# Moving the two widest score blocks of a pair of heads between the two turns of the pair before it

## The chip, the cores and the metric

The kernel runs on one core of a Trainium2 chip. The metric is the device time of one execution in microseconds (us), smaller is better. The time of the kernel before is the median of three runs.

## The reference

The program computes two blocks of a transformer on 512 tokens of width 1024, in fp32. The first block projects the normalised input, runs two attentions of eight heads each on parts of the projection, multiplies their outputs by a gate and projects them back. The second block is four layers, each with an attention and a feed-forward part; the change does not touch it. Cut to the first block's attentions:

```python
def chunk_causal_attention(q, k, v, pos):        # heads of "phase 1", width 96
    def block(args):
        logits = jnp.einsum('bqhd,bshd->bhqs', qb, k).astype(jnp.float32) * scale
        mask = pos[None, :] < chunk_limit(pb)[:, None]
        logits = jnp.where(mask[None, None], logits, NEG_INF)
        p = jax.nn.softmax(logits, axis=-1).astype(v.dtype)
        return jnp.einsum('bhqs,bshd->bqhd', p, v)
...
def indexer_sparse_attention(q, k, v, q_idx, k_idx, w_idx, pos):   # heads of "phase 2", width 64
    ...
        _, sel = lax.top_k(score, topk)          # each query keeps 128 keys
    ...
        logits = jnp.where(valid[:, None], logits, NEG_INF)
        p = jax.nn.softmax(logits, axis=-1).astype(v.dtype)
        return jnp.einsum('bhqk,bqkhd->bqhd', p, v_sel)
...
    mixed = jnp.concatenate([o_a.reshape(B, S, A_WIDTH) * jax.nn.silu(g_a),
                             o_b.reshape(B, S, B_WIDTH) * jax.nn.silu(g_b)], axis=-1)
    h = h + mixed @ w_out[l]
```

## The kernel before

Every engine runs a program of its own, in an order written out by hand, and the engines wait for each other through counting semaphores. An engine never skips an instruction that waits: what stands behind it waits too.

The first block's attention (`attn`) works on eight pairs of heads, p = 0 to 7. Pairs 0 to 3 are phase 1, pairs 4 to 7 (`p >= PAIRS_B`) phase 2. In phase 2 the two heads j = 0, 1 of a pair lie in the two halves of the partitions of one tile `qp` and one tile `kp`, and the mask of chosen keys is added to the scores. A pair passes through these steps:

1. `prep` (TensorE, L723): four transposes of queries and four of keys into two banks of PSUM. VectorE (`take_heads`, L1965) scales them out of PSUM into `qp` and `kp`.
2. `scores` (TensorE, L767): eight blocks, for each 128 queries i = 0 to 3 and each head j; block i is 128 (i + 1) keys wide. In phase 2 they come in the order of i, j = 0 and j = 1 next to each other. VectorE (L1996, shown as `e<-ring,mask`) adds the mask, takes the maximum of each row and writes the block to SBUF as `e_1[p % 2][j]`.
3. `exps` (ScalarE, L1426): exp of each of the eight blocks, with the sum of each row. VectorE (`take_reciprocal`, L2003) inverts the sums of head j once its blocks are through. Head 0 is scaled by VectorE itself (`normalise`, L2009, four instructions), head 1 by GpSimd (L1143, four instructions).
4. `turn(p, j)` (TensorE, L931): ten transposes of head j's scaled blocks into the PSUM tile `turn`. ScalarE (`take_turned`, L1433) copies them to SBUF as `at_1[j]`. There is one tile `turn`, so the next turn waits for this copy.
5. `pv` (TensorE, L783): the sum over keys, for both heads, into the PSUM tile `out`. VectorE (`gate`, L2017) multiplies it by the gate into `ot`; ScalarE (`out_high`, L1437) rounds that to `o1h`; VectorE (`low`, L2022) makes the rest, `o1l`.

Steps of different pairs are interleaved. In step s of the loop TensorE does `scores(s)`, `pv(s-2)`, `turn(s-1, 0)`, `prep(s+1)`, `turn(s-1, 1)`. VectorE does the score blocks of s, `take_reciprocal(s, 0)`, `normalise(s)`, `take_prep(s+1)`, `take_reciprocal(s, 1)`, `low(s-3)`, `gate(s-2)`. ScalarE does `exps(s)`, `take_turned(s-1, 0)`, `out_high(s-3)`, `take_turned(s-1, 1)`.

PSUM banks are handed out by a ring of four, `ring[n % 4]`, where n is the number of a unit: a score block or half a prep, numbered in the order of `pair_units()`. TensorE may write unit n once VectorE has taken unit n - 4:

```python
    def wait_unit_free(b, k):
        if b.at("unit_taken", k) >= 4:
            pe.wait_ge(m["unit_taken"], b.at("unit_taken", k) - 3)
```

So the fifth block of a pair waits until VectorE has taken its first.

After the last pair's scores there is nothing left to interleave but the output projection. `work.fill(n)` issues n quanta of it, each of three matmuls 512 columns wide (L472); a quantum k needs `low(k)`. In step 8 TensorE does `pv(6)`, `turn(7, 0)`, five quanta, `turn(7, 1)`, six quanta, and in step 9 `pv(7)` and then all other quanta.

Of the kernel before, what the change touches and what calls it, by code (L numbers as in the profile page):

```python
# [101 lines left out]
PAIRS = 8  # L102
PAIRS_B = B_HEADS // 2
# [8 lines left out]


def pair_preps(p):


    return [(x, j) for j in range(2 if p < PAIRS_B else 1) for x in ("q", "k")]


def pair_units():  # L120
    order = [("gate", 6), ("prep", 0, *pair_preps(0)[-1]), ("gate", 7)]
    for p in range(PAIRS):
        order += [("score", p, *u) for u in pair_scores(p)]
        if p + 1 < PAIRS:
            order += [("prep", p + 1, *u) for u in pair_preps(p + 1)]
    return {u: n for n, u in enumerate(order)}

# [348 lines left out]
def tensor_program(pe, m, st, plan):  # L476
# [269 lines left out]
    def attn(b, ob):  # L746
# [9 lines left out]

        def scores(p):
            taken = UNITS[("prep", p, *pair_preps(p)[-1])] + 1 if p else 0
            pe.wait_ge(m["unit_taken"], b.at("unit_taken", taken))
            for j, i in pair_scores(p):  # L760
                if p < PAIRS_B:
                    q, k = m.qp[j][0:B_QK, :], m.kp[j][0:B_QK, :]
                else:
                    half = slice(64 * j, 64 * j + 64)
                    q, k = m.qp[0][half, :], m.kp[0][half, :]
                n = CAUSAL_W[i]
                pe.matmul(bank(("score", p, j, i))[:, 0:n], q[:, i * P:(i + 1) * P], k[:, 0:n],  # L767
                          start=True, stop=True).then_inc(m["unit_ready"], 1)
# [21 lines left out]
        for s in range(PAIRS + 2):  # L790
            if s < PAIRS:
                scores(s)
            if s >= 2:
# [3 lines left out]
            if s + 1 < PAIRS:  # L797
                if s + 1 == PAIRS_B:
                    pe.wait_ge(m["q_normed"], 4)
                prep(s + 1)  # L800
            elif s == PAIRS:
                work.fill(5)
            if 1 <= s < PAIRS + 1:
# [292 lines left out]
    for name in plan:  # L1096
        b = st[name]
# [111 lines left out]
def scalar_program(act, m, d, st, plan, n_pieces):  # L1209
# [211 lines left out]
    def attn(b):  # L1421
        def exps(p):
            for j, i in pair_scores(p):
                act.wait_ge(m["unit_taken"], b.at("unit_taken", UNITS[("score", p, j, i)] + 1))
# [18 lines left out]
        for s in range(PAIRS + 3):  # L1443
            if s >= PAIRS:
                out_high(s - 3)
            if s < PAIRS:
                exps(s)
            if 1 <= s < PAIRS + 1:
                take_turned(s - 1, 0)
            if 3 <= s < PAIRS:  # L1450
                out_high(s - 3)
            if 1 <= s < PAIRS + 1:
                take_turned(s - 1, 1)
# [199 lines left out]
def vector_program(dve, m, st, plan):  # L1653
# [303 lines left out]
    def take_heads(b, unit, p, x, j):  # L1957
        dst = (m.qp if x == "q" else m.kp)[j]
        wait_unit(b, unit)
# [27 lines left out]
    def attn(b):  # L1987
        def scores(p):

            for j, i in pair_scores(p):  # L1990
                if p >= 2:
# [23 lines left out]
        def gate(p):  # L2015
            dve.wait_ge(m["pv_done"], b.at("pv_done", p + 1))
            dve.tensor_tensor(m.ot[p % 2][:], m.out[:], m.gate[:, (p + 4) % 8, :], ALU.mult).then_inc(m["o_taken"], 1)  # L2017

# [12 lines left out]
        for s in range(PAIRS + 3):  # L2031
            if s < PAIRS:
                scores(s)
            if s >= PAIRS:
                low(s - 3)
            if s == 0:

                take_prep(1)
                make_mask()
            if s < PAIRS:  # L2040
                take_reciprocal(s, 0)
                normalise(s)
            if 1 <= s < PAIRS - 1:
                take_prep(s + 1)
            if s < PAIRS:
                take_reciprocal(s, 1)
            if 3 <= s < PAIRS:
                low(s - 3)
            if 2 <= s < PAIRS + 2:
                gate(s - 2)  # L2050
# [502 lines left out]
```

## Time and profile before

| what | value |
| --- | --- |
| median of 3 runs | 2704.96 us |
| lowest and highest | 2703.01 and 2705.85 us |
| the profiled execution's own time | 2703.59 us |
| its span, first to last instruction | 2701.8 us |
| TensorE busy | 2653.8 us (98%) |
| VectorE, ScalarE, GpSimd busy | 1456.8, 1116.9, 1168.1 us |
| phase 2 of the attention in the span | about 268 to 310 us |

Busy time is the time in which the profiler saw an instruction of the engine at work. A matmul's end is modelled, and successive matmuls overlap, so where two matmuls follow without a wait, the distance of their starts is the time that one takes. In a timeline the number in brackets is how long the engine sat idle before the row, and the name behind the arrow is what ended that. PE is TensorE, DVE VectorE, ACT ScalarE, POOL GpSimd. Names of tiles stand without their numbers.

### The profile page before, as it was taken

Reading aid. Unit: us, or ns where it says so; the run is one execution under the profiler, and the core shown is the slowest. Engines: PE = TensorE matmul, PEld = TensorE weight load, DVE = VectorE, ACT = ScalarE, POOL = GpSimd, SP = SyncE. Lnnn points to the kernel's source line nnn. Section 1 sums busy time; section 2 is a strip of 40 time slices with the busy share of each in tenths; the row PEclk is TensorE's granted clock in tenths of the full one; section 3 lists DMA queues with packets and bytes.
Section 4 is the critical chain, followed back from the end, with each engine's and each line's share of the span. In section 5 each row is a group of like instructions: output and inputs, shape, how many; then the busy total and the mean of one; then the engine's idle time right before and its main releaser. Section 6 shows DMA issues by size and latency. Waiting matters only on the chain.

```text
span 2701.8 us, 32030 instructions
## 1 busy us (share of the span) xinstructions
PE 2653.8 (98%) x12868; PEld 2124.2 (79%) x12868; DVE 1456.8 (54%) x2610; ACT 1116.9 (41%) x1509; POOL 1168.1 (43%) x880
## 2 busy tenths in 40 slices
PE   8999999999999999999999999999999999999997
PEld 7786677778888877778888876888888777888886
DVE  5888556657554145657554145575522565565522
ACT  4545544443333236654333236443332444443331
POOL 3454343335445532335445541354455332454453
PEclk9999999999999999999999999999999999999999
DMA  4224032222223321112323331222233221222232
GB/s 163 78 94 172 10 124 86 78 79 94 94 94 109 110 83 62 63 63 96 107 94 109 109 110 48 79 94 105 98 110 109 95 85 71 94 94 96 106 111 78
DMA packets 45605, 253.44 MB, mean 94 GB/s; under 512 B 4560, under 2 KB 9184, under 8 KB 17936
## 3 DMA queue, kind: packets, MB, share of 16 engines
q1 hardware_dynamic: 34656, 232.18, 24.5%
q10 hardware_dynamic: 10800, 19.20, 2.1%
q8 instruction: 102, 1.67, 0.2%
q14 instruction: 47, 0.39, 0.0%
HBM read 249.21 MB, written 10.55 MB: 96 GB/s over the span
## 4 chain that ended last, share of the span: by engine, by line
PE 92%; DVE 4%; ACT 2%; POOL 1%; issue 1%; DMA 0%; SPq 0%; DVEq 0%; ACTq 0%
PE ring L472 78%; PE ring L926 3%; PE turn L931 2%; PE turn L472 1%; PE out L970 1%; POOL wlo L1166 1%; PE ring L636 1%; PE ring L767 1%; PE out L783 1%; DVE sp L2158 1%; PE out L976 0%; DVE e L2126 0%; PE out L1058 0%; DVE z L2161 0%; ACT whi L1217 0%
## 5 line engine op out<-in xcount | busy, mean ns | idle before, releaser
L1166 POOL TENSOR_TENSOR wlo<-raw,whi 128x512 fp32r<-128x512 f32 x840 | 1122.8, 1369 | 1461.2 <-ACT whi L1217 1461.2
L472 PE MATMUL ring<-xh,whi 128*128 128x512 f32 x1888 | 753.0, 399 | 9.1 <-DVE xl L1673 8.2
L472 PE MATMUL ring<-xh,wlo 128*128 128x512 f32 x1888 | 736.4, 390 | 0.0
L472 PE MATMUL ring<-xl,whi 128*128 128x512 f32 x1888 | 736.2, 390 | 0.0
L1217 ACT ACTIVATE whi<-raw 128x2048 fp32r<-128x2048 f32 x215 | 411.3, 1914 | 435.4 <-DMA raw<-in_pieces 419.9
L472 PEld LDWEIGHTS ring<-xh,whi 128*128 128x128 f32 x1888 | 354.9, 188 | 114.3 <-issue 40.9
L472 PEld LDWEIGHTS ring<-xh,wlo 128*128 128x128 f32 x1888 | 354.9, 188 | 74.9
L472 PEld LDWEIGHTS ring<-xl,whi 128*128 128x128 f32 x1888 | 355.1, 188 | 72.6 <-issue 3.4
L2274 DVE SCALAR_TENSOR_TENSOR taps<-u,conv,taps 128x511 f32<-128x511 f32 (+1 forms) x344 | 294.5, 900 | 18.4 <-ACT taps L1615 16.0
L2288 DVE TENSOR_TENSOR u<-ring,r 128x512 f32<-128x512 f32 x168 | 114.4, 687 | 300.9 <-PE ring L472 300.9
L2262 DVE TENSOR_TENSOR h<-ring,h 128x512 f32<-128x512 f32 x72 | 49.6, 689 | 420.0 <-PE ring L852 376.9
L1615 ACT ACTIVATE taps<-u,conv 128x512 f32<-128x512 f32 x172 | 137.9, 809 | 306.6 <-DVE u L2288 306.4
L472 PE MATMUL ring<-hh,whi 128*128 128x512 f32 x672 | 261.4, 389 | 0.0
L472 PE MATMUL ring<-hl,whi 128*128 128x512 f32 x672 | 261.4, 389 | 0.0
L472 PE MATMUL ring<-hh,wlo 128*128 128x512 f32 x672 | 261.4, 389 | 0.0
L472 PE MATMUL ring<-whi,xh 128*128 128x256 f32 (+1 forms) x576 | 181.6, 315 | 1.3 <-POOL wlo L1166 1.3
L472 PE MATMUL ring<-wlo,xh 128*128 128x256 f32 (+1 forms) x576 | 173.6, 301 | 0.0
L472 PE MATMUL ring<-whi,xl 128*128 128x256 f32 (+1 forms) x576 | 173.6, 301 | 0.0
L472 PEld LDWEIGHTS ring<-hl,whi 128*128 128x128 f32 x672 | 126.2, 188 | 26.2
L472 PEld LDWEIGHTS ring<-hh,wlo 128*128 128x128 f32 x672 | 126.2, 188 | 26.2
L472 PEld LDWEIGHTS ring<-hh,whi 128*128 128x128 f32 x672 | 126.1, 188 | 26.2
L472 PEld LDWEIGHTS ring<-whi,xh 128*128 128x128 f32 x576 | 110.4, 192 | 21.1 <-issue 13.9
(285 smaller groups left out, 3355.0 us busy)
## 6 DMA issues: line engine op xcount, KB each, us to landing
raw<-in_pieces SPq DMA_DIRECT2D x215, 1024.0 KB, 4.7
toep<-diag_store ACTq DMA_DIRECT2D x16, 512.0 KB, 3.6
diag_store<-diag_row ACTq DMA_DIRECT2D x1, 5120.0 KB, 25.2
band_store<-band_row ACTq DMA_DIRECT2D x1, 3072.0 KB, 32.5
h<-in_x SPq DMA_DIRECT2D x4, 512.0 KB, 6.7
wbias<-band_store ACTq DMA_DIRECT2D x4, 512.0 KB, 7.4
result<-h SPq DMA_DIRECT2D x8, 256.0 KB, 2.2
raw<-in_pieces SPq DMA_DIRECT2D x4, 256.0 KB, 6.9
```

The lines of the kernel that those rows point to most:

```text
L472: ins = pe.matmul(out, stationary, moving, start=first and n == 0, stop=last and n == 2)
L636: ins = pe.matmul(out, x[:, tok], weights[slot][:, w], start=begins, stop=ends)
L767: pe.matmul(bank(("score", p, j, i))[:, 0:n], q[:, i * P:(i + 1) * P], k[:, 0:n], start=True, stop=True).then_inc(m["unit_ready"], 1)
L783: ins = pe.matmul(m.out[64 * j:64 * j + 64, kk * P:S], v[:, kk, c:c + 64], m.at_1[j][:, at:at + S - kk * P], start=kk == 0, stop=kk == TT - 1)
L926: pe.matmul(m.ring[2 + j][:, 0:n], qs[part, i * P:(i + 1) * P], ks[part, lo:lo + n], start=True, stop=True).then_inc(m["su_ready"], 1)
L931: ins = pe.transpose(m.turn[:, to:to + P], src[:, at:at + P], m.ident[:])
L1166: ins = pool.tensor_tensor(m.wlo[slot][:, part], m.raw[slot][:, part], m.whi[slot][:, part].bitcast(F32), ALU.subtract)
L1217: act.activation(m.whi[p % SLOTS][:], m.raw[p % SLOTS][:], ACT.Copy).then_inc(m["hi_done"], 1)
L1615: act.activation(taps[g][:], m.u[g][:], ACT.Identity, scale=cols[:, 4 * g + 2:4 * g + 3], bias=cols[:, 4 * g + 3:4 * g + 4]).then_inc(m["t ...
L2262: dve.tensor_tensor(m.h[:, k, :], ring(b, k)[:], m.h[:, k, :], ALU.add).then_inc(m["unit_taken"], 1)
L2274: dve.scalar_tensor_tensor(y[:, shift:S], m.u[g][:, 0:S - shift], cols[:, tap:tap + 1], y[:, shift:S], ALU.mult, ALU.add).then_inc(m[signa ...
L2288: dve.tensor_tensor(m.u[g][:], ring(b, 2 * t + g)[:], m.r[:], ALU.mult).then_inc(m["unit_taken"], 1)
```

## The change

In phase 2 a pair's eight score blocks are split. The first six (128, 256 and 384 keys wide) stay where they were, the last two (512 keys wide, "the late blocks") move behind `prep(s+1)` on TensorE, ahead of `turn(s-1, 1)`. The units are numbered anew to match. Queries and keys of odd pairs of phase 2 go to a second place, `qp[1]` and `kp[1]`, since `prep(s+1)` is now taken while scores of s are still to be made. ScalarE's two late exps move between its two copies. On VectorE `gate(s-2)` and `take_prep(s+1)` move ahead of the late blocks, and so ahead of `take_reciprocal(s, 0)` and `normalise(s)`. In step 8 two of the five quanta move ahead of `pv(6)`. `gate` names a semaphore that VectorE's own order has met already.

```diff
--- before.py
+++ after.py
@@ -111,6 +111,16 @@
     return [(j, i) for i in range(TT) for j in range(2)]
 
 
+def first_scores(p):
+
+
+    return pair_scores(p)[:8 if p < PAIRS_B else 6]
+
+
+def late_scores(p):
+    return pair_scores(p)[len(first_scores(p)):]
+
+
 def pair_preps(p):
 
 
@@ -120,9 +130,10 @@
 def pair_units():
     order = [("gate", 6), ("prep", 0, *pair_preps(0)[-1]), ("gate", 7)]
     for p in range(PAIRS):
-        order += [("score", p, *u) for u in pair_scores(p)]
+        order += [("score", p, *u) for u in first_scores(p)]
         if p + 1 < PAIRS:
             order += [("prep", p + 1, *u) for u in pair_preps(p + 1)]
+        order += [("score", p, *u) for u in late_scores(p)]
     return {u: n for n, u in enumerate(order)}
 
 
@@ -754,15 +765,15 @@
             for x, j in pair_preps(p):
                 turn_heads(bank(("prep", p, x, j)), p, x, j)
 
-        def scores(p):
+        def scores(p, blocks):
             taken = UNITS[("prep", p, *pair_preps(p)[-1])] + 1 if p else 0
             pe.wait_ge(m["unit_taken"], b.at("unit_taken", taken))
-            for j, i in pair_scores(p):
+            for j, i in blocks:
                 if p < PAIRS_B:
                     q, k = m.qp[j][0:B_QK, :], m.kp[j][0:B_QK, :]
                 else:
                     half = slice(64 * j, 64 * j + 64)
-                    q, k = m.qp[0][half, :], m.kp[0][half, :]
+                    q, k = m.qp[p % 2][half, :], m.kp[p % 2][half, :]
                 n = CAUSAL_W[i]
                 pe.matmul(bank(("score", p, j, i))[:, 0:n], q[:, i * P:(i + 1) * P], k[:, 0:n],
                           start=True, stop=True).then_inc(m["unit_ready"], 1)
@@ -789,7 +800,9 @@
         gate(b, UNITS[("gate", 7)], 0, 1)
         for s in range(PAIRS + 2):
             if s < PAIRS:
-                scores(s)
+                scores(s, first_scores(s))
+            if s == PAIRS:
+                work.fill(2)
             if s >= 2:
                 pv(s - 2)
             if 1 <= s < PAIRS + 1:
@@ -799,7 +812,9 @@
                     pe.wait_ge(m["q_normed"], 4)
                 prep(s + 1)
             elif s == PAIRS:
-                work.fill(5)
+                work.fill(3)
+            if s < PAIRS and late_scores(s):
+                scores(s, late_scores(s))
             if 1 <= s < PAIRS + 1:
                 turn(s - 1, 1)
             if s == PAIRS:
@@ -1419,8 +1434,8 @@
         take(11)
 
     def attn(b):
-        def exps(p):
-            for j, i in pair_scores(p):
+        def exps(p, blocks):
+            for j, i in blocks:
                 act.wait_ge(m["unit_taken"], b.at("unit_taken", UNITS[("score", p, j, i)] + 1))
                 row = m.e_1[p % 2][j][:, BLOCK_OFF[i]:BLOCK_OFF[i] + CAUSAL_W[i]]
                 act.activation(row, row, ACT.Exp, bias=m.nmax[:, p % 2, j, i:i + 1], scale=-1.0,
@@ -1444,11 +1459,13 @@
             if s >= PAIRS:
                 out_high(s - 3)
             if s < PAIRS:
-                exps(s)
+                exps(s, first_scores(s))
             if 1 <= s < PAIRS + 1:
                 take_turned(s - 1, 0)
             if 3 <= s < PAIRS:
                 out_high(s - 3)
+            if s < PAIRS:
+                exps(s, late_scores(s))
             if 1 <= s < PAIRS + 1:
                 take_turned(s - 1, 1)
 
@@ -1955,7 +1972,7 @@
                 pick_round(8 + (unit if unit[0] == "gate" else GATES[n - 1])[1])
 
     def take_heads(b, unit, p, x, j):
-        dst = (m.qp if x == "q" else m.kp)[j]
+        dst = (m.qp if x == "q" else m.kp)[j if p < PAIRS_B else p % 2]
         wait_unit(b, unit)
         if p < PAIRS_B:
             gain = m.cols[0:B_QK, C_HEAD + (x == "k"):C_HEAD + (x == "k") + 1]
@@ -1985,9 +2002,9 @@
         own.settle()
 
     def attn(b):
-        def scores(p):
-
-            for j, i in pair_scores(p):
+        def scores(p, blocks):
+
+            for j, i in blocks:
                 if p >= 2:
                     dve.wait_ge(m["turned"], b.at("turned", 2 * p - 2 if p >= PAIRS_B else 2 * (p - 2) + j + 1))
                 k, n = UNITS[("score", p, j, i)], CAUSAL_W[i]
@@ -2014,6 +2031,8 @@
 
         def gate(p):
             dve.wait_ge(m["pv_done"], b.at("pv_done", p + 1))
+            if p >= 2:
+                dve.wait_ge(m["ol_ready"], b.at("ol_ready", p - 1))
             dve.tensor_tensor(m.ot[p % 2][:], m.out[:], m.gate[:, (p + 4) % 8, :], ALU.mult).then_inc(m["o_taken"], 1)
 
         def low(p):
@@ -2030,23 +2049,28 @@
         dve.wait_ge(m["gate_ready"], 8)
         for s in range(PAIRS + 3):
             if s < PAIRS:
-                scores(s)
+                scores(s, first_scores(s))
             if s >= PAIRS:
                 low(s - 3)
             if s == 0:
 
                 take_prep(1)
                 make_mask()
+            if PAIRS_B <= s < PAIRS:
+                gate(s - 2)
+                if s < PAIRS - 1:
+                    take_prep(s + 1)
+                scores(s, late_scores(s))
             if s < PAIRS:
                 take_reciprocal(s, 0)
                 normalise(s)
-            if 1 <= s < PAIRS - 1:
+            if 1 <= s < PAIRS_B:
                 take_prep(s + 1)
             if s < PAIRS:
                 take_reciprocal(s, 1)
             if 3 <= s < PAIRS:
                 low(s - 3)
-            if 2 <= s < PAIRS + 2:
+            if 2 <= s < PAIRS_B or PAIRS <= s < PAIRS + 2:
                 gate(s - 2)
 
     def take_v(b, unit, v, half):
```

**VectorE, from pair 4's blocks of 384 keys to pair 5's first block, before.** `e_100` and `e_101` are heads 0 and 1 of an even pair, `e_110` and `e_111` of an odd one; `o1l5` is `low` of pair 1 and `ot0` is `gate` of pair 2.

```order
L1996 ISA e_101_156,nmax_123<-ring3,mask_154 128x384
...
L1996 ISA e_100_155,nmax_123<-ring0,mask_154 128x512
...
L1996 ISA e_101_156,nmax_123<-ring1,mask_154 128x512
...
L2003 RECIPROCAL rl_125<-lsum_124 128x4
...
L2009 TENSOR_SCALAR e_100_155<-e_100_155,rl_125 128x512
L1965 TENSOR_SCALAR qp0_133<-ring2 128x512
L1965 TENSOR_SCALAR kp0_135<-ring3 128x512
L2003 RECIPROCAL rl_125<-lsum_124 128x4
L2022 TENSOR_TENSOR o1l5_174<-ot1_144,o1h5_166 128x512
L2017 TENSOR_TENSOR ot0_143<-out,gate_86 128x512
L1996 ISA e_110_157,nmax_123<-ring0,mask_154 128x128
```

After the change:

```order
L2013 ISA e_101_156,nmax_123<-ring3,mask_154 128x384
...
L2036 TENSOR_TENSOR ot0_143<-out,gate_86 128x512
L1982 TENSOR_SCALAR qp1_134<-ring0 128x512
L1982 TENSOR_SCALAR kp1_136<-ring1 128x512
L2013 ISA e_100_155,nmax_123<-ring2,mask_154 128x512
...
L2013 ISA e_101_156,nmax_123<-ring3,mask_154 128x512
...
L2020 RECIPROCAL rl_125<-lsum_124 128x4
...
L2026 TENSOR_SCALAR e_100_155<-e_100_155,rl_125 128x512
L2020 RECIPROCAL rl_125<-lsum_124 128x4
L2041 TENSOR_TENSOR o1l5_174<-ot1_144,o1h5_166 128x512
L2013 ISA e_110_157,nmax_123<-ring0,mask_154 128x128
```

The two instructions that take queries and keys (`qp`, `kp`) and the gate (`ot0`) now stand ahead of the late blocks. Between the late blocks and the next pair's first block stand the two reciprocals, the scaling and `low`, and nothing else.

**TensorE, from pair 4's turn of head 0 to pair 6's first block, before.** `e_100` and `e_101` are pair 4's heads, `at_10` and `at_11` their turned copies.

```order
L931 MATMUL turn<-ident_62,e_100_155 128x128 x10
L723 MATMUL ring0<-ident_62,q_a_82 128x128 x4
L723 MATMUL ring1<-ident_62,k_a_83 128x128 x4
L931 MATMUL turn<-ident_62,e_101_156 128x128 x10
L767 MATMUL ring2<-kp0_135,qp0_133 128x128
L767 MATMUL ring3<-kp0_135,qp0_133 128x128
```

After, at the same place; here the two rows of L778 with 512 columns are pair 5's late blocks:

```order
L946 MATMUL turn<-ident_62,e_100_155 128x128 x10
L734 MATMUL ring2<-ident_62,q_a_82 128x128 x4
L734 MATMUL ring3<-ident_62,k_a_83 128x128 x4
L778 MATMUL ring0<-kp1_136,qp1_134 128x512
L778 MATMUL ring1<-kp1_136,qp1_134 128x512
L946 MATMUL turn<-ident_62,e_101_156 128x128 x10
L778 MATMUL ring2<-kp0_135,qp0_133 128x128
L778 MATMUL ring3<-kp0_135,qp0_133 128x128
```

The late blocks stand between the two turns, and pair 6's queries and keys go to a place that pair 5's late blocks don't read.

**TensorE, from pair 6's turn of head 0 to pair 7's turn of head 1, before.** Rows of L472 are quanta of the output projection, three rows each; between the first and last `out` rows lie `pv(6)`'s others.

```order
L931 MATMUL turn<-ident_62,e_100_155 128x128 x10
L931 MATMUL turn<-ident_62,e_101_156 128x128 x10
L783 MATMUL out<-at_10_159,v_a_84 64x512
...
L783 MATMUL out<-at_11_160,v_a_84 64x128
L931 MATMUL turn<-ident_62,e_110_157 128x128 x10
L472 MATMUL ring0<-o1h4_165,whi0_55 128x512
L472 MATMUL ring0<-o1l4_173,whi0_55 128x512
...
L472 MATMUL ring0<-o1h0_161,wlo0_58 128x512
L931 MATMUL turn<-ident_62,e_111_158 128x128 x10
```

After:

```order
L946 MATMUL turn<-ident_62,e_100_155 128x128 x10
L778 MATMUL ring2<-kp1_136,qp1_134 128x512
L778 MATMUL ring3<-kp1_136,qp1_134 128x512
L946 MATMUL turn<-ident_62,e_101_156 128x128 x10
L483 MATMUL ring0<-o1h4_165,whi0_55 128x512
...
L483 MATMUL ring0<-o1h5_166,wlo0_58 128x512
L794 MATMUL out<-at_10_159,v_a_84 64x512
...
L794 MATMUL out<-at_11_160,v_a_84 64x128
L946 MATMUL turn<-ident_62,e_110_157 128x128 x10
L483 MATMUL ring0<-o1h6_167,whi0_55 128x512
...
L483 MATMUL ring0<-o1h0_161,wlo0_58 128x512
L946 MATMUL turn<-ident_62,e_111_158 128x128 x10
```

Two late blocks now stand between the turns of pair 6, and two quanta ahead of `pv(6)`; three quanta are left between the turns of pair 7.

## Rows read from the trace of the kernel before

**Rows 1.** The page: its head, and the chain that ended last, by engine.

```profile
span 2701.8 us, 32030 instructions
...
PE 92%; DVE 4%; ACT 2%; POOL 1%; issue 1%; DMA 0%; SPq 0%; DVEq 0%; ACTq 0%
```

**Rows 2.** TensorE's timeline, 284 to 322 us: start, length, engine, line, operation, idle.

```profile
290.20 2.38 PE L783 MATMUL out<-at,v_a 128*64 128x512 f32 x16
292.50 1.31 PE L931 MATMUL turn<-ident,e 128*128 128x128 f32 x10
293.65 0.60 PE L723 MATMUL ring<-ident,q_a 128*128 128x128 f32 x4
294.08 0.60 PE L723 MATMUL ring<-ident,k_a 128*128 128x128 f32 x4
295.14 1.31 PE L931 MATMUL turn<-ident,e 128*128 128x128 f32 x10 [0.45 <-ACT at L1433]
...
301.63 1.31 PE L931 MATMUL turn<-ident,e 128*128 128x128 f32 x10
304.27 1.31 PE L931 MATMUL turn<-ident,e 128*128 128x128 f32 x10 [1.33 <-ACT at L1433]
306.91 2.38 PE L783 MATMUL out<-at,v_a 128*64 128x512 f32 x16 [1.33 <-ACT at L1433]
...
310.28 0.47 PE L472 MATMUL ring<-o1h,whi 128*128 128x512 f32 x1
...
313.81 1.25 PE L931 MATMUL turn<-ident,e 128*128 128x128 f32 x10
```

**Rows 3.** The timeline of all engines, 287 to 290.3 us, same columns.

```profile
287.88 0.29 DVE L1996 CUSTOM_DVE_ANT_0 e<-ring,mask 128x128 f32<-128x128 f32 x1
...
288.23 1.21 PEld L767 LDWEIGHTS ring<-kp,qp 64*128 64x128 f32 x8 [0.46 <-DVE nmax L1996]
...
289.29 0.56 DVE L1996 CUSTOM_DVE_ANT_0 e<-ring,mask 128x384 f32<-128x384 f32 x1 [0.20 <-PE ring L767]
```

**Rows 4.** The timeline of VectorE, 285 to 304 us, same columns.

```profile
286.50 0.69 DVE L2022 TENSOR_TENSOR o1l<-ot,o1h 128x512 fp32r<-128x512 f32 x1
287.11 0.68 DVE L2017 TENSOR_TENSOR ot<-out,gate 128x512 f32<-128x512 f32 x1
...
292.27 0.18 DVE L2003 RECIPROCAL rl<-lsum 128x4 f32<-128x4 f32 x1 [0.72 <-ACT e L1426]
...
297.01 0.29 DVE L1996 CUSTOM_DVE_ANT_0 e<-ring,mask 128x128 f32<-128x128 f32 x1
...
301.40 0.18 DVE L2003 RECIPROCAL rl<-lsum 128x4 f32<-128x4 f32 x1 [0.72 <-ACT e L1426]
...
302.81 0.17 DVE L2003 RECIPROCAL rl<-lsum 128x4 f32<-128x4 f32 x1
```

**Rows 5.** The timeline of ScalarE, 285 to 317 us, same columns.

```profile
291.44 0.71 ACT L1426 ACTIVATE e<-e,nmax 128x512 f32<-128x512 f32 x1
...
302.98 1.24 ACT L1433 ACTIVATE at<-turn 128x1280 f32<-128x1280 f32 x1 [0.91 <-PE turn L931]
304.12 0.62 ACT L1437 ACTIVATE o1h<-ot 128x512 fp32r<-128x512 f32 x1
```

**Rows 6.** The timeline of all engines, 260 to 262.4 us, same columns.

```profile
260.85 0.69 DVE L1996 CUSTOM_DVE_ANT_0 e<-ring,chunk 128x512 f32<-128x512 f32 x1 [0.29 <-PE ring L767]
...
261.58 0.72 ACT L1426 ACTIVATE e<-e,nmax 128x512 f32<-128x512 f32 x1 [0.28 <-DVE nmax L1996]
```

**Rows 7.** The timeline of GpSimd, 301 to 310 us, same columns.

```profile
303.07 4.27 POOL L1143 TENSOR_SCALAR e<-e,rl 128x128 f32<-128x128 f32 x4 [2.60 <-DVE rl L2003]
```

**Rows 8.** The timeline of TensorE, 104 to 109 us, same columns.

```profile
104.70 0.47 PE L636 MATMUL ring<-whi,ct_h 128*128 128x512 f32 x1 [1.27 <-issue]
```

**Rows 9.** Busy time by stretch: bounds, length, each engine's busy us, granted clock, DMA.

```profile
107.40:110.90 3.50, 3.50 (x12) 2.85 (x11) 2.82 (x7) 0.85 (x4) 0.00 (x0) 0.51 0.00 0
...
302.00:309.00 7.00, 4.34 (x33) 2.80 (x33) 3.18 (x7) 3.59 (x5) 4.27 (x4) 1.00 0.00 0
```

## The prediction

> **What bounds the kernel now.** I read the page first: TensorE holds 92% of the chain that ended last [rows 1], so what this stretch gains or loses reaches the end in full, if TensorE is what gains or loses. Then the timeline of TensorE over phase 2, to find where it stands still. A step there is 9.13 us long (from one pair's first block on VectorE to the next pair's, 287.88 and 297.01) [rows 3, 4]. TensorE stands still twice in it: 0.45 us ahead of the turn of head 1, for ScalarE's copy of head 0 [rows 2], and 0.46 us ahead of the pair's fifth score block, for VectorE to take the first one and free its bank [rows 3]. Past the last pair's scores nothing lies between the turns and two waits for the copy stand open, 1.33 us each [rows 2]. Last I read VectorE's timeline for what it does around its waits. The first stall and the last two are what late blocks and quanta can cover; the second one hangs on where VectorE stands when a pair begins, and that is what the change moves.
>
> **The change part by part.** Nothing is added but the second place for queries and keys, which costs no instruction. The count on every engine stays; only order and waits move. So the cost is that of the new loop of waits.
>
> *From a pair's late blocks to the next pair's fifth block.* I follow one step from L, the start of the late blocks on TensorE.
> - To VectorE's work on the first late block. The fifth block, 384 wide, takes 1.06 from TensorE's start (288.23) to VectorE's (289.29) [rows 3]. `pv` makes 1280 columns for two heads side by side in 2.30 (290.20 to 292.50), 0.23 per 128 columns [rows 2]. A block's matmul is made in two passes over its columns. With 128 columns more it lands between 1.06 (none of them counts) and 1.29 (all 0.23 do); I take the middle, 1.17.
> - VectorE to ScalarE's exp of that block: 0.73, from a place where ScalarE stood waiting for exactly this (260.85 to 261.58) [rows 6].
> - exp to the reciprocal of head 0: 0.83 (291.44 to 292.27) [rows 4, 5].
> - Reciprocal, four scalings, reciprocal of head 1: 1.41 (301.40 to 302.81), the second reciprocal 0.17 [rows 4]. The exp of head 1 starts 0.71 after the first [rows 5] and is ready in time.
> - `low`: 0.61 to the next instruction (286.50 to 287.11); from an instruction of this form to a score block it is 0.77 (287.11 to 287.88) [rows 3, 4]. I take 0.70.
> - The next pair's first block on VectorE to TensorE's fifth: 0.35 (287.88 to 288.23) [rows 3].
>
> Together 1.17 + 0.73 + 0.83 + 1.41 + 0.17 + 0.70 + 0.35 = 5.36 us. TensorE needs from L only the late blocks (4 x 0.23 = 0.92), the turn of head 1 (1.15, as 292.50 to 293.65) and the next pair's four small blocks (128, 128, 256, 256 wide, heads side by side: 3 x 0.23 = 0.69) [rows 2]: it arrives at 2.8 and stands still for some 2.5 us. Behind it in TensorE's queue is `pv`, so nothing fills that.
>
> *From the fifth block to the next late blocks.* Before, the eight-block sequence takes 1.97 from the fifth block to `pv` (288.23 to 290.20) [rows 2, 3]: 0.69 for the 384-wide pair, 0.92 for the 512-wide one, and 0.36 for banks that come free one by one. The 512-wide pair leaves this place; I leave the 0.36 here: 1.05 (bounds 0.69 and 1.1). Then `pv` 2.30, the turn of head 0 1.15, two halves of prep at 0.43 (293.65 to 294.08) [rows 2]: 1.05 + 2.30 + 1.15 + 0.86 = 5.36.
>
> So the new period is 5.36 + 5.36 = 10.72 us against 9.13: 1.59 more. The loop closes three times, from pair 4 to 5, 5 to 6 and 6 to 7; pair 4 begins as before, since the step ahead of it is not changed. 3 x 1.59 = +4.77 us at the start of pair 7. The 0.45 wait for the copy is gone, covered by the late blocks, and it gains nothing: it lay inside a step that is now as long as the chain through VectorE.
>
> Other waits inside the step, counted from F, the pair's first block on VectorE. ScalarE begins the copy of head 0 1.35 after its turn starts (301.63 to 302.98), then `out_high` 1.14 later and 0.62 long [rows 2, 5], so it is free at 0.35 + 1.05 + 2.30 + 1.35 + 1.14 + 0.62 = 6.81; the late exp is wanted at 0.35 + 5.36 + 1.17 + 0.73 = 7.61. Hidden in steps 4 to 6. GpSimd's scaling of head 1 starts 0.26 after its reciprocal and takes 4.27 here [rows 4, 7]; it would be through well ahead of its turn, a step later. Both have room only because the step is longer.
>
> *The tail, from F of pair 7.* The turn of pair 6's head 0 starts at 0.35 + 1.05 + 2.30 = 3.70, the late blocks (no prep now) at 4.85, VectorE has them at 6.02, the exp could start at 6.75, ScalarE is free at 6.81. The second exp starts 0.71 later and is done, with its row sums, 0.83 after that: 8.35. Only then can ScalarE copy the turn of head 1, and `pv(6)` follows 1.29 after the copy's start (302.98 to 304.27, the same distance from copy to TensorE) [rows 2, 5]: 9.64. Before it is 306.91 - 297.01 = 9.90 [rows 2, 4]. So two waits of 1.33 are filled with 0.92 and two quanta, and of that just 0.26 shows ahead of `pv(6)`, since the copy itself is now late. The two quanta count behind it: five take 3.53 (310.28 to 313.81) [rows 2], so 2 x 0.71 = 1.41 less work remains. The tail gives 0.26 + 1.41 = 1.67. The three quanta left between pair 7's turns, 2.12, still cover a copy of 1.35. GpSimd's scaling for pair 7 ends near 6.81 + 0.83 + 1.41 + 0.26 + 4.27 = 13.6, its turn comes near 15: no wait.
>
> *The sum.* +4.77 - 1.67 = +3.1 us. The profiled execution, 2703.59 us, would become 2706.7; it lies 1.4 below the median of its three runs, 2704.96, so for the median I say 2708.1.
>
> **What hides what, and the clock.** A stall of 2.5 us is longer than any that TensorE has in phase 2 now. The trace shows the granted clock at 0.51, that is 1.2 GHz, from 107.4 to 110.9 after a 1.27 us gap at 103.4 with thin work behind it [rows 8, 9]; yet over 302 to 309, with two gaps of 1.33 and 4.34 of 7 us busy, it stayed at 1.00, 2.4 GHz [rows 2, 9]. So gaps alone don't decide here and the new stall lies on the unsafe side of both. The Trainium skill, page "TensorE: Matmul & The Clock Gate", section "Why this matters for your kernels", puts the danger at idle gaps longer than this one would be; by it the clock holds and the sum stays +3.1. The drop at 107.4 does not fit that rule. A drop of 3.5 us at half speed costs up to 1.7 us where TensorE's own work is on the chain, and half of the new period is TensorE's.
>
> **Rivals.**
> 1. *The clock falls behind one or more of the three stalls.* Each costs between 0.9 and 1.7 us: one gives 2709.4, three up to 2713.2. For it: the gap at 104.70. Against it: 302 to 309 [rows 2, 8, 9].
> 2. *The other side: the stall does not form, and the covered waits show.* It takes VectorE reaching the next pair's first block early enough, that is the path of 5.36 us down to TensorE's 2.8. Then a step loses its 0.45 and 0.46: 3 x 0.91 = 2.7, one more 0.45 in step 4, and the tail of 1.67: -4.9, so 2700.1 us. The point from which it decides: the total is nil when the path is 1.0 us shorter, 4.3 us (3 x 1.0 = 3.1), and faster below. For it: VectorE idles 0.72 per step for exps now [rows 4], a sign of some room. Against it: each piece is a measured distance with its wait in place, and none looks 1 us too long.
> 3. *ScalarE or GpSimd becomes the wait as well.* If ScalarE got to the late exps as late in each step as in pair 7, nothing changes, it has 0.8 us of room (7.61 - 6.81); were the copies 1 us later the period would grow by 0.2, in all +0.6: 2708.7. Little speaks for it.
>
> **How the numbers follow.** A change of under 0.2% (5.4 us) is about what this kernel's measurement can't tell from none; the three runs spread over 2.8 us. Chances: the stall with the clock held 63%, with a clock drop 22%, rival 2 in full or part 10%, rival 3 5%. With the bounds of the steps (1.06 or 1.29; 0.61 or 0.77; 0.69 or 1.1) the period lies between 10.2 and 11.0, the total between +1.4 and +4, and with the spread of medians the likeliest case by itself spans 2706.0 to 2709.6. The range of 8 in 10 adds one or two drops above and a partly smaller stall below: 2704.6 to 2711.6. Slower by over 0.2% (2710.4) needs two drops, 0.15; faster by over 0.2% (2699.5) needs more than rival 2, 0.03.
>
> **What would show each step.** In the changed profile: a period of 10.7 in phase 2 between first blocks of pairs on VectorE; TensorE idle some 2.5 us ahead of the fifth block of pairs 5, 6 and 7, ended by VectorE's row maximum; no wait ahead of the turn of head 1 in steps 4 to 6; VectorE idle twice around the late blocks, ended by TensorE and by ScalarE's exp; `pv(6)` still waiting about 0.7 for ScalarE's copy. It is wrong if the period is below 9.5, or if the stall stands at another block.

## The result, and the profile after

The changed kernel takes 2709.88 us in the median of 22 runs (2707.28 to 2715.25), the one before 2705.30 us in the median of 22 runs on the same chips (2700.96 to 2708.90). The ratio is 1.0018, with a 95% interval of 1.0012 to 1.0024: slower by about 4.9 us (3.2 to 6.5). That is clear of zero, and small: 0.18% of the time. The profiled execution took 2711.00 us. From the page, its head and the chain by engine:

```profile
span 2709.2 us, 32040 instructions
...
PE 92%; DVE 4%; ACT 2%; POOL 1%; issue 1%; DMA 0%; DVEq 0%; SPq 0%; ACTq 0%
```

The chain's shares are those of before [rows 1], so they don't show the difference; the timelines do. Here is TensorE over one step of the changed kernel, from pair 4's first block to pair 5's `pv`. L778 are score blocks, L946 turns, L734 preps, L794 `pv`.

```profile
269.99 2.11 PE L778 MATMUL ring<-kp,qp 64*128 64x128 f32 x12
272.02 2.38 PE L794 MATMUL out<-at,v_b 128*64 128x512 f32 x16
274.33 1.31 PE L946 MATMUL turn<-ident,e 128*128 128x128 f32 x10
275.48 0.60 PE L734 MATMUL ring<-ident,q_a 128*128 128x128 f32 x4
...
276.44 1.13 PE L778 MATMUL ring<-kp,qp 64*128 64x512 f32 x4
277.50 1.31 PE L946 MATMUL turn<-ident,e 128*128 128x128 f32 x10
278.74 1.03 PE L778 MATMUL ring<-kp,qp 64*128 64x128 f32 x8
281.71 1.75 PE L778 MATMUL ring<-kp,qp 64*128 64x384 f32 x4 [1.93 <-DVE nmax L2013]
283.39 3.38 PE L794 MATMUL out<-at,v_b 128*64 128x512 f32 x16
```

The late blocks stand at 276.44, between prep and the turn of head 1, and the wait of 0.45 us ahead of that turn [rows 2] is gone. Pair 5's four small blocks start at 278.74. Then TensorE idles 1.93 us by its matmuls, until VectorE has taken the first block. The 0.46 at this place before [rows 3] was read from the record of the weight loads, where the same wait is now 2.33:

```profile
281.71 0.61 PEld L778 LDWEIGHTS ring<-kp,qp 64*128 64x128 f32 x4 [2.33 <-DVE nmax L2013]
```

VectorE in the same step:

```profile
270.62 0.29 DVE L2013 CUSTOM_DVE_ANT_0 e<-ring,mask 128x128 f32<-128x128 f32 x1
...
277.71 0.69 DVE L2013 CUSTOM_DVE_ANT_0 e<-ring,mask 128x512 f32<-128x512 f32 x1 [0.31 <-PE ring L778]
...
279.30 0.18 DVE L2020 RECIPROCAL rl<-lsum 128x4 f32<-128x4 f32 x1 [0.27 <-ACT e L1441]
...
280.70 0.17 DVE L2020 RECIPROCAL rl<-lsum 128x4 f32<-128x4 f32 x1
280.78 0.66 DVE L2041 TENSOR_TENSOR o1l<-ot,o1h 128x512 fp32r<-128x512 f32 x1
281.36 0.28 DVE L2013 CUSTOM_DVE_ANT_0 e<-ring,mask 128x128 f32<-128x128 f32 x1
```

and ScalarE's first late exp:

```profile
278.45 0.72 ACT L1441 ACTIVATE e<-e,nmax 128x512 f32<-128x512 f32 x1 [1.01 <-DVE nmax L2013]
```

This is the loop of the prediction, row by row: late block on TensorE 276.44, on VectorE 277.71, its exp 278.45, the reciprocal 279.30, the second reciprocal 280.70, `low` 280.78, the next pair's first block 281.36, TensorE's fifth block 281.71. Pair 4's first block stood at 270.62, so the period is 10.74 us.

The next two periods are 12.38 each (first blocks at 281.36, 293.74, 306.12), 1.64 more. In the step of pair 5 the time from the fifth block to `pv` is 1.68 us (281.71 to 283.39) instead of 1.05, and `pv` takes 3.3 us instead of 2.3; in the step of pair 6 `pv` alone takes 3.9 (295.14 to 299.08). Busy time by stretch, the granted clock in the column before the last two:

```profile
278.70:282.10 3.40, 1.47 (x12) 1.02 (x12) 3.10 (x14) 2.80 (x8) 1.14 (x2) 0.99 0.00 0
282.10:285.50 3.40, 3.40 (x10) 0.98 (x10) 1.50 (x8) 2.76 (x11) 3.40 (x3) 0.50 0.00 0
...
295.70:299.10 3.40, 3.40 (x17) 1.31 (x13) 0.49 (x4) 1.43 (x6) 2.26 (x2) 0.50 0.00 0
```

For 3.4 us from 282.1 and again from 295.7 the clock is granted at 0.50, the level of 1.2 GHz. TensorE had been busy 1.47 of the 3.4 us ahead of the first fall.

The two traces differ ahead of this stretch too: from 238 to 241 us the clock of the changed kernel stood at 0.50 and that of before at 1.00, and pair 4's first block comes at 270.62 instead of 269.61. So the stretch from that block on is compared, and not the whole span.

The tail, TensorE from the turn of pair 6's head 0:

```profile
309.82 1.31 PE L946 MATMUL turn<-ident,e 128*128 128x128 f32 x10
311.06 1.13 PE L778 MATMUL ring<-kp,qp 64*128 64x512 f32 x4
312.46 1.31 PE L946 MATMUL turn<-ident,e 128*128 128x128 f32 x10 [0.27 <-ACT at L1448]
...
315.76 2.38 PE L794 MATMUL out<-at,v_a 128*64 128x512 f32 x16 [0.60 <-ACT at L1448]
...
326.63 2.37 PE L794 MATMUL out<-at,v_a 128*64 128x512 f32 x16
```

The two waits of 1.33 us [rows 2] are down to 0.27 and 0.60. `pv(6)` comes 9.64 us behind pair 7's first block (306.12) and `pv(7)` 10.87 behind `pv(6)`; before it was 9.90, and 12.22 (306.91 to 319.13).

The places that all runs are compared by, in us, each from its own timelines of VectorE and TensorE. F is the first block of a pair on VectorE; the last column counts the falls of the clock between F of pair 4 and `pv(7)`.

| kernel | F of pair 4 to 5, 5 to 6, 6 to 7 | F of 7 to pv(6) | pv(6) to pv(7) | F of 4 to pv(7) | clock falls |
| --- | --- | --- | --- | --- | --- |
| before | 9.13, 9.14, 9.13 | 9.90 | 12.22 | 49.52 | 0 |
| changed | 10.74, 12.38, 12.38 | 9.64 | 10.87 | 56.01 | 2 |
| changed, again | 10.74, 12.38, 10.74 | 11.33 | 10.86 | 56.05 | 2 |
| spare matmuls | 10.75, 10.74, 10.74 | 9.64 | 10.86 | 52.73 | 0 |
| low later | 10.17, 10.13, 10.13 | 9.62 | 10.86 | 50.91 | 0 |
| next pair first | 8.79, 9.12, 9.12 | 9.97 | 10.85 | 47.85 | 0 |
| copy between | 8.80, 9.41, 9.16 | 9.91 | 11.63 | 48.91 | 0 |
| last pair only | 9.13, 9.14, 9.13 | 9.66 | 10.85 | 47.91 | 0 |
| quanta only (both runs) | 9.13, 9.13, 9.14 | 9.90 | 10.85 | 48.15 | 0 |
| scores only | 10.75, 10.74, 12.37 | 9.64 | 13.96 | 57.46 | 2 |

### The profile page after: what moved, and what is told of

Its sections match the earlier page's. It is cut to its first block, busy times and chain, and to the rows that moved or that the text cites. A ratio compares the mean times of both kernels' runs of the same rounds, so it can differ in the third digit from the quotient of the medians.

```text
span 2709.2 us, 32040 instructions
## 1 busy us (share of the span) xinstructions
PE 2658.9 (98%) x12868; PEld 2124.5 (78%) x12868; DVE 1459.5 (54%) x2610; ACT 1117.8 (41%) x1509; POOL 1168.3 (43%) x880
## 3 DMA queue, kind: packets, MB, share of 16 engines
q8 instruction: 102, 1.67, 0.2%
## 4 chain that ended last, share of the span: by engine, by line
PE 92%; DVE 4%; ACT 2%; POOL 1%; issue 1%; DMA 0%; DVEq 0%; SPq 0%; ACTq 0%
PE ring L483 78%; PE ring L941 3%; PE turn L946 2%; PE turn L483 1%; PE out L985 1%; POOL wlo L1181 1%; PE ring L778 1%; PE ring L647 1%; PE out L794 1%; DVE sp L2182 1%; PE out L991 0%; DVE e L2150 0%; PE out L1073 0%; DVE z L2185 0%; ACT whi L1232 0%
## 5 line engine op out<-in xcount | busy, mean ns | idle before, releaser
L1635 ACT ACTIVATE taps<-taps 128x512 f32<-128x512 f32 x88 | 55.7, 633 | 175.5 <-DVE taps L2298 175.5
```

The lines of the kernel that those rows point to most:

```text
L1635: act.activation(taps[0][0:rows, :], taps[0][0:rows, :], ACT.Silu).then_inc(m["silu"], 1)
```

## Experiments

Theory A is the prediction's: a loop of waits from a pair's late blocks through VectorE, ScalarE's exp and VectorE again to the next pair's fifth block. Its rivals are named in each expectation. Distances in the traces repeat to 0.02 us where the order is the same and the clock holds, while whole runs of one kernel spread over some 8 us. So a cause is read from the traces, and the ratio says what it is worth.

**The next pair's blocks first.** VectorE's order alone is altered (cut to the main place):

```diff
             if s < PAIRS:
-                scores(s, first_scores(s))
+                scores(s, first_scores(s)[2 if s > PAIRS_B else 0:])
...
             if s < PAIRS:
                 take_reciprocal(s, 0)
+            if PAIRS_B <= s < PAIRS:
+                if s + 1 < PAIRS:
+                    scores(s + 1, first_scores(s + 1)[:2])
+                take_reciprocal(s, 1)
+            if s < PAIRS:
                 normalise(s)
...
```

> The changed kernel, with VectorE's order altered alone: behind a pair's late blocks it inverts the sums of head 0, takes the next pair's first two blocks, inverts the sums of head 1, and only then scales head 0 and makes low. Theory A (the stall is VectorE's order: reciprocal, scaling and low ahead of the next pair's first block): the fifth block can start 1.17 + 0.73 + 0.83 + 0.22 + 0.35 = 3.3 us after the late blocks instead of 5.36, TensorE gets there at 2.8 to 2.9, so the stall falls from 2.3 to some 0.4 us and the period from 10.7 to 8.7 us, under the 9.13 of before; in all 3 x -0.43 and the tail's -1.7, about -3.0 us against before, and no fall of the clock in phase 2. Theory B (the late blocks themselves are what costs, by TensorE's work or by the banks, whatever VectorE does): the period stays above 10 us and the time some 3 us above before.

Ratio to before 0.9997 (0.9988 to 1.0005), median 2703.61 us. TensorE with its weight loads, then VectorE, then ScalarE, in the step of pair 7:

```profile
293.22 1.13 PE L778 MATMUL ring<-kp,qp 64*128 64x512 f32 x4
...
295.52 2.15 PE L778 MATMUL ring<-kp,qp 64*128 64x128 f32 x12
297.92 2.38 PE L794 MATMUL out<-at,v_a 128*64 128x512 f32 x16 [0.25 <-ACT at L1448]
```

```profile
296.54 0.51 PEld L778 LDWEIGHTS ring<-kp,qp 64*128 64x128 f32 x4 [0.39 <-DVE nmax L2013]
```

```profile
295.10 0.69 DVE L2013 CUSTOM_DVE_ANT_0 e<-ring,mask 128x512 f32<-128x512 f32 x1
...
296.07 0.18 DVE L2020 RECIPROCAL rl<-lsum 128x4 f32<-128x4 f32 x1 [0.27 <-ACT e L1441]
296.19 0.29 DVE L2013 CUSTOM_DVE_ANT_0 e<-ring,mask 128x128 f32<-128x128 f32 x1
```

```profile
295.94 0.71 ACT L1441 ACTIVATE e<-e,nmax 128x512 f32<-128x512 f32 x1
...
296.65 1.21 ACT L1448 ACTIVATE at<-turn 128x1280 f32<-128x1280 f32 x1
```

The wait ahead of the fifth block fell from 2.33 to 0.39 us by the weight loads, as expected, and the period from 10.74 to 9.12 (8.79 in the first step). So theory A holds and B is out: with the late blocks left where they are, VectorE's order alone takes the loss away. The size was missed, 9.12 for 8.7. TensorE now waits 0.25 us ahead of `pv` for ScalarE's copy, which stands behind both late exps: exp at 295.94, copy at 296.65, `pv` at 297.92. This is a second loop, through ScalarE: from the late blocks to `pv` 4.70 us (293.22 to 297.92), from `pv` to the next late blocks 4.42 (288.80 to 293.22), together the 9.12. It was close behind the first, and the expectation had not summed it.

**`low` later.** `low(s - 4)` goes ahead of `gate(s - 2)`, and the old place is left out but for the last pair:

```diff
             if PAIRS_B <= s < PAIRS:
+                if s > PAIRS_B:
+                    low(s - 4)
                 gate(s - 2)
...
-            if 3 <= s < PAIRS:
+            if 3 <= s < PAIRS_B or s == PAIRS - 1:
                 low(s - 3)
```

> The changed kernel with low of a pair moved behind the next pair's first six blocks on VectorE, ahead of the gate. Theory A (every VectorE instruction between the late blocks and the next pair's first block is on the loop, at its full length): the period falls by 0.58 us, from 10.74 to 10.16, the stall from 2.3 to 1.7; in all 1.7 us less than the changed kernel, +1.3 to +1.5 against before if the clock holds, up to +3 if it falls once. Theory B: VectorE's order is not the limit, no change against the changed kernel (+4.6).

Ratio 1.0009 (1.0000 to 1.0018), median 2706.74 us. TensorE around the stall:

```profile
288.07 1.03 PE L778 MATMUL ring<-kp,qp 64*128 64x128 f32 x8
290.43 1.12 PE L778 MATMUL ring<-kp,qp 64*128 64x384 f32 x4 [1.33 <-DVE nmax L2013]
```

The period is 10.13 to 10.17 and the wait 1.33: an instruction of 0.58 us taken off the loop gave 0.57 to 0.61 of period and 0.60 of stall. From F of pair 4 to `pv(7)` it is 1.39 us over before, as expected, with no fall of the clock in this trace.

**Spare matmuls in the stall.** They compute nothing that is used; `pv` overwrites them.

```diff
             for j, i in blocks:
+                if p > PAIRS_B and (j, i) == (0, 2):
+                    pe.wait_ge(m["o_taken"], b.at("o_taken", p - 2))
+                    for _ in range(2):
+                        pe.matmul(m.out[:], m.ident[:], m.chunk[:], start=True, stop=True)
```

> The changed kernel with two spare matmuls of 512 columns (0.92 us each by pv's rate) on TensorE ahead of the fifth block of pairs 5, 6 and 7, into the tile out, which pv overwrites. They lie inside the stall of 2.3 us. Theory A (the clock falls because of the stall, and this is the part of the loss beyond 3.1 us): no stretch at 0.50 in phase 2, all three periods at 10.7 us, time about 3.0 us above before instead of 4.6. Theory B (the falls have another cause, such as thin work around the stall): stretches at 0.50 stay, time 4.6 above before. If the spare matmuls don't fit in the stall the period grows by what sticks out.

Ratio 1.0012 (1.0003 to 1.0021), median 2707.97 us. TensorE at pair 5's stall, and the busy time and granted clock of the next two steps:

```profile
278.71 1.03 PE L782 MATMUL ring<-kp,qp 64*128 64x128 f32 x8
279.67 1.98 PE L775 MATMUL out<-chunk,ident 128*128 128x512 f32 x4
281.68 1.12 PE L782 MATMUL ring<-kp,qp 64*128 64x384 f32 x4
```

```profile
282.00:292.70 10.70, 10.67 (x66) 6.15 (x65) 7.52 (x27) 7.42 (x20) 4.56 (x5) 1.00 0.00 0
292.70:303.40 10.70, 10.68 (x66) 6.16 (x66) 7.53 (x27) 7.42 (x20) 4.58 (x5) 1.00 0.01 3
```

The spare matmuls lie in the stall and delay nothing: the fifth block starts 2.97 us behind the first (278.71 to 281.68), as in the changed kernel (278.74 to 281.71). The clock stays at 1.00 and all three periods are 10.74. This is the changed kernel with the clock held: 52.73 against 49.52, +3.2 us. That the spare matmuls are what held it rests on one trace, and since only five of the nine bare stalls traced have a fall behind them (below), three without one could also be chance. The medians point the same way: 2707.97 us here, 2709.88 and 2710.17 with the bare stall, though the intervals of their ratios overlap.

**The changed kernel once more.**

> The changed kernel itself once more, for a second trace and for more runs on the chip of these comparisons. Theory A (the stall of 1.9 to 2.3 us ahead of the fifth block of pairs 5 to 7 is the same in every execution, and whether the clock falls behind it differs from one execution to the next): the same three stalls, between none and three stretches at 0.50 in phase 2, each making its period up to 1.7 us longer than 10.74. Theory B (the falls belong to the order of the program): again two, behind the stalls of pairs 5 and 6.

Ratio 1.0021 (1.0013 to 1.0030), median 2710.17 us. The stretches at the lower clock in its trace:

```profile
281.40:284.80 3.40, 3.40 (x11) 1.00 (x10) 1.19 (x6) 2.37 (x10) 3.17 (x3) 0.50 0.00 0
...
305.30:308.70 3.40, 3.40 (x16) 1.46 (x12) 0.62 (x4) 1.56 (x6) 2.39 (x2) 0.50 0.00 0
```

Again two falls, but behind the stalls of pairs 5 and 7, where the first trace had them behind 5 and 6. So theory A holds: which stall is hit changes from one execution to the next; the stalls themselves don't. A fall makes its period 12.38 instead of 10.74, 1.64 us; behind pair 7's stall it makes `pv(6)` come at 11.33 instead of 9.64, 1.69 us.

**The last pair only.** Pair 7 alone has late blocks (`[:6 if p == PAIRS - 1 else 8]`), with VectorE's and ScalarE's moves in its step alone, and the quanta of the change.

> The change for the last pair alone: only pair 7 has late blocks, and two quanta stand ahead of pv(6); pairs 4 to 6 as before. Theory A (the steps lose, the tail gains, by separate sums): phase 2 runs as before up to pair 7's first block, and the tail gives -1.7 us: ratio 0.9994. Theory B (the loss lies anywhere that a late pair stands): slower than before by about a third of the loss, +1.5 us.

Ratio 0.9996 (0.9987 to 1.0005), median 2703.73 us. The three periods are those of before to 0.01 us, and from F of pair 7 to `pv(7)` it is 20.51 instead of 22.12: -1.61. The steps lose and the tail gains, by sums that don't touch each other.

**The quanta only, and the scores only.** The first is the kernel before with `work.fill(2)` ahead of `pv(6)` and `fill(3)` behind, the second the changed kernel without that:

```diff
+            if s == PAIRS:
+                work.fill(2)
             if s >= 2:
                 pv(s - 2)
...
             elif s == PAIRS:
-                work.fill(5)
+                work.fill(3)
```

> The kernel before with one part of the change: two of the five quanta ahead of pv(6). Theory A: the wait of 1.33 us for ScalarE's copy ahead of pv(6) is filled, pv(6) starts within 0.1 us of where it did, and pv(7) starts 1.3 us earlier behind pair 7's first block on VectorE (22.12 before, 20.8). Theory B: the quanta only push pv(6) back and nothing is gained.

> The kernel before with two quanta ahead of pv(6), timed this time; in its one execution so far pv(7) came 20.75 us behind pair 7's first block instead of 22.12. Theory A (a wait of 1.33 us on TensorE's chain filled, nothing else moved): 1.3 to 1.4 us less than before, ratio 0.9995. Theory B (something later takes it back): ratio 1.0000.

> The changed kernel with all five quanta behind the turn as before. Theory A: pv(6) starts where it does in the changed kernel (9.64 behind pair 7's first block), now with a wait of some 2.0 us ahead of it, and pv(7) starts 1.4 us later than in the changed kernel (21.9 behind pair 7's first block, against 22.12 before). So the late blocks alone give the tail 0.2 to 0.3 us. Theory B: without the quanta pv(6) comes earlier than 9.64, because they delay it.

Of the quanta only there are two traces and a series of runs, of the scores only one execution and so no ratio. With the quanta alone the ratio is 0.9998 (0.9989 to 1.0007), median 2703.80 us. Its TensorE at the turn of pair 6's head 1 and at `pv(6)`:

```profile
303.80 1.31 PE L933 MATMUL turn<-ident,e 128*128 128x128 f32 x10 [1.33 <-ACT at L1435]
...
306.44 2.37 PE L783 MATMUL out<-at,v_a 128*64 128x512 f32 x16
```

`pv(6)` waits no more, starts where it did, and `pv(7)` comes 1.37 us earlier, in both traces. With the scores alone `pv(6)` waits:

```profile
313.41 4.06 PE L794 MATMUL out<-at,v_a 128*64 128x512 f32 x16 [1.99 <-ACT at L1446]
```

It starts 9.64 behind pair 7's first block with or without the quanta, so they don't delay it. This `pv` ran at the lower clock, from 313.9 (it takes 4.0 us), so the 13.96 to `pv(7)` holds a fall of 1.7; without it 12.3, about as before, and the late blocks alone give the tail some 0.2 to 0.3, all of it ahead of `pv(6)`.

**The copy between the late exps**, on top of the kernel with the next pair's blocks first:

```diff
             if s < PAIRS:
-                exps(s, late_scores(s))
+                exps(s, late_scores(s)[:1])
             if 1 <= s < PAIRS + 1:
                 take_turned(s - 1, 1)
+            if s < PAIRS:
+                exps(s, late_scores(s)[1:])
```

> The kernel in which VectorE takes the next pair's first two blocks early, with one more change of order: ScalarE copies the turn of head 1 between its two late exps instead of behind both. That kernel's period was 9.12 us, with TensorE waiting 0.25 us for this copy ahead of pv. Theory A (with VectorE's order mended the loop runs late blocks, two exps, copy, pv: 1.17 + 0.73 + 0.71 + 0.8 + 1.29 + 2.30 + 1.15 + 0.86 = 9.0 us): the copy starts 0.8 earlier, the wait ahead of pv goes, the period falls to 8.7 to 8.9 us, pv(6) comes 0.66 us earlier behind pair 7's first block (9.64 to 9.0), and the time is 1.5 to 2 us below that kernel and 2.5 to 3.5 below before. Theory B: head 1's sums now come later, GpSimd's scaling (4.6 us) becomes the wait ahead of the turn of head 1, and the period stays at 9.1.

Ratio 0.9997 (0.9988 to 1.0006), median 2704.18 us. ScalarE and TensorE in one step:

```profile
291.79 0.51 ACT L1441 ACTIVATE e<-e,nmax 128x256 f32<-128x256 f32 x1 [1.64 <-DVE nmax L2015]
...
293.99 1.22 ACT L1448 ACTIVATE at<-turn 128x1280 f32<-128x1280 f32 x1
...
296.60 1.24 ACT L1448 ACTIVATE at<-turn 128x1280 f32<-128x1280 f32 x1
```

```profile
291.68 1.31 PE L946 MATMUL turn<-ident,e 128*128 128x128 f32 x10
...
295.25 1.31 PE L946 MATMUL turn<-ident,e 128*128 128x128 f32 x10 [0.33 <-ACT at L1448]
```

Neither theory as written. The wait ahead of `pv` is gone, but behind a first period of 8.80 the next are 9.41 and 9.16. The reciprocal of head 1, now behind a later exp, holds up the scaling, `low` and the next pair's third block on VectorE; ScalarE waits 1.64 us for that block (291.79) and comes to the copy of head 0 only at 293.99, 2.3 us behind the turn's start at 291.68 instead of 1.35, and the turn of head 1 waits for it. GpSimd shows as a wait too, but only once, 0.59 us ahead of pair 7's turn of head 1.

**Four late blocks**, an attempt at an order in which each of these waits is covered: two more blocks late, `low` ahead of the next pair's first two blocks, its other two behind the scaling, `out_high` first.

> A version made from what the runs so far showed: in phase 2 four late blocks instead of two (384 and 512 wide, both heads), so that the four first ones need no bank that VectorE must free in the same step; VectorE takes the next pair's first two blocks ahead of the reciprocals, the other two behind the scaling, low ahead of them, the gate at the step's start; ScalarE makes out_high first, and the copy of the turn of head 1 between the third and the fourth late exp; three quanta ahead of pv(6), three and five behind. Theory A (TensorE stood only for waits that this order can cover: for a bank, and for the copies): the period falls to 9.5 us or less in the first steps and below 9 later, from pair 4's first block to pv(7) it takes 45.3 us by the sums against 49.5 before, so about 4 us less than before, ratio 0.9985. Theory B (ScalarE, with exps of 4.4, two copies of 1.14 and 0.6 in a step of 9.1, is the next limit whatever the order, as the run with the copy between the exps suggested): 47.5 to 48.5, as with the next pair's blocks first, ratio 0.9994.

Ratio 1.0003 (0.9994 to 1.0012), median 2704.53 us. TensorE at two `pv` in a row:

```profile
289.48 2.38 PE L794 MATMUL out<-at,v_a 128*64 128x512 f32 x16 [0.61 <-ACT at L1448]
...
298.74 2.38 PE L794 MATMUL out<-at,v_a 128*64 128x512 f32 x16 [0.61 <-ACT at L1448]
```

The period is 9.26 (289.48 to 298.74) and the wait for ScalarE's copy stands at 0.61. So theory A is out: ScalarE's copy is the wait in this order too. That it would be so whatever the order, as theory B says, is not shown: ScalarE is busy 7.46 of these 9.26 us, so its work would fit a shorter step. The distance that I had summed, from pair 4's first block to `pv(7)`, came out at 44.27 us, below what either theory gave, and was the wrong one to compare: in this order pair 4's first block itself stands behind a gate that waits for `pv(2)`, and comes late. From `pv(1)` to `pv(7)` it takes 54.88 us, before 56.34: a gain of 1.46, less than the last pair alone gives.

## Why the prediction was right, point by point

- *The loop from late blocks to the next pair's fifth block*, put at 5.36 us, measured 276.44 to 281.71: 5.27. To VectorE 1.27 (1.17 was said), to the exp 0.74 (0.73), to the reciprocal 0.85 (0.83), to the second reciprocal 1.40 (1.41), `low` 0.08 behind it (0.17) and 0.58 to the next block (0.70), to TensorE 0.35 (0.35). The stall itself is 2.33 us by the weight loads and 1.93 by the matmuls; 2.5 was said, with TensorE arriving at 2.8 us; it arrives at 3.0.
- *From the fifth block to the next late blocks*, put at 5.36, measured 5.47 where the clock held: 1.05, 2.31, 1.15 and 0.96 for the two halves of prep (0.86 was said). Period 10.74 against the 10.72 predicted: so close because one half came out 0.09 short and the other 0.11 long, which is luck. The mechanism is not: that each part of the loop counts in full is shown by `low` later, and that the loop is VectorE's order by the next pair first.
- *The tail*: `pv(6)` at 9.64, as predicted to the hundredth, but by errors that cancel. The first late exp starts at 6.95 (313.07) for VectorE's sake and not at 6.81, when ScalarE is free, and the copy follows the second exp's start by 0.71 and not by 0.83. The gain is 1.61 against 1.67; the quanta alone give 1.37 and the late blocks alone 0.26 ahead of `pv(6)`.
- *The sum*: +3.1 predicted, +3.2 measured with the clock held, in the trace with the spare matmuls.
- *The clock* was the step that was off. It stood as a rival with 22% and the price of 0.9 to 1.7 a fall, and the likeliest case had the clock held. All three traces of kernels with the bare stall of 1.93 us have two falls in this stretch; none of the others has one there. The price is 1.63 to 1.70 each. The measured ratio, +4.9 us, leaves 1.7 for them beside the 3.2, one fall on average. That is reckoned and not counted: 3.2 to 6.5 us allows from none to two, and both traces of the changed kernel have two. So 2709.9 lies in the range, but by rival 1 rather than by the forecast case; 2705.3 and 3.2 alone, 2708.5, would lie in it as well. The Trainium skill's rule (page "TensorE: Matmul & The Clock Gate", section "Why this matters for your kernels") names longer idle gaps than this one of 1.93 us as the danger; with a fall behind five of nine such gaps the measurement decides against it here.
- *Rival 2*, the side on which the kernel gets faster, needed VectorE to reach the next pair early. The next pair first made nearly that, and the gain it gave, 1.67 us from F of pair 4 to `pv(7)`, is far from the 4.9 of that rival. It left out ScalarE's copy as the next wait, the loop of 9.12 us. And it added up 0.45 and 0.46 as if both were TensorE's to win. The chain that ended last, in the kernel before, leaves TensorE behind prep and comes back at the next pair's fifth block:

```profile
292.57 1.24 PE turn L931 x10
293.81 0.45 PE ring L723 x4
294.29 0.69 DVE qp L1965
...
296.33 0.60 DVE ot L2017
...
297.36 2.04 PE ring L767 x8
```

  It passes by the turn of head 1, so by this chain covering the 0.45 ahead of that turn could only have made the wait ahead of the fifth block longer.
- *Open*: whether a fall costs less in a step with more room, and what the mean number of falls per execution is; only the traced ones are counted. None of the versions beats before by more than the runs can tell, though the traces of next pair first, last pair only and the quanta show 1.67, 1.61 and 1.37 us less.

## What to carry to other kernels

When a piece of work is moved later on the engine that is the bound, follow what it must pass through on the others before the next piece of the same kind can start; here 0.45 us of cover bought a loop of 10.7 us in a step of 9.1. Sum that loop, and the second and third longest too: each mended order ended at another wait, at a period of 9.1 to 9.4. And price a stall by the clock that it may lose as well as by its length.

## What the runs showed of the hardware that was not expected

An idle stretch of 1.93 us on TensorE, with score blocks of half the partitions on either side, was followed by a fall of the granted clock to 0.50 for 3.4 us in five of nine such places in three traces, and once behind a wait of 1.99 us ahead of `pv`; the gaps of 1.33 us in the traces of before and of `low` later were followed by none. Outside this stretch one of 1.27 us before 104.70 was followed by 0.51 from 107.4 on [rows 8, 9], though TensorE was busy all the time between, so the length of the gap alone does not decide. Two spare matmuls of 0.92 us in that place went with a clock of 1.00 in all three steps of the one trace taken, and with 3.3 us less of the traced 56.0, though they compute nothing.
